# A mixture-of-experts stage on one core: gate and up from split weights to plain fp32, and the context tokens of down on four partition groups

## What is computed

```python
def ec_moe(h, w_router, w_gate, w_up, w_down):
    ...
    cap = EC_CAPACITY_FACTOR * t // N_EXPERTS
    gates, idx = lax.top_k(aff.T, cap)
    xs = ht[idx]
    a = jnp.einsum('ecd,edf->ecf', xs, w_gate)
    u = jnp.einsum('ecd,edf->ecf', xs, w_up)
    y = jnp.einsum('ecf,efd->ecd', jax.nn.silu(a) * u, w_down) * gates[..., None].astype(h.dtype)
    out = jnp.zeros((t, d), h.dtype).at[idx.reshape(-1)].add(y.reshape(-1, d))
```

## Time and profile before

| what | value |
|---|---|
| median of 3 runs | 3486.37 us (3486.07 to 3488.76) |
| profiled execution, span | 3480.6 us |
| PE busy / DVE busy / POOL busy | 3166.9 / 2532.4 / 1483.4 us |
| first transpose of the expert stage | 874.4 us |
| last matmul of the expert stage | 3431.0 us |
| mean granted TensorE clock | 0.949 |

### The profile page before, as it was taken

How to read it: one execution, slowest core, us unless ns; L and a number is a source line. 1 busy time by engine, 2 the same in 40 slices (tenths; PEclk the granted TensorE clock), 3 DMA queues, 4 the chain that set the end, 5 groups by cost and what they waited for, 6 DMA issues and landing times. The chain is left out here.

```text
span 3480.6 us, 50738 instructions
## 1 busy us (share of the span) xinstructions
PE 3166.9 (91%) x19191; PEld 2741.1 (79%) x19191; DVE 2532.4 (73%) x3014; ACT 1278.2 (37%) x2046; POOL 1483.4 (43%) x860
## 2 busy tenths in 40 slices
PE   8999989894899999989898999999898989999994
PEld 2699987683788888878787888888787878888883
DVE  2343331225789898988898898989898989889895
ACT  2222221232334434434343344343434343434432
POOL 2233330123345455453545454544535354535443
PEclk9999999996899999999999999999999999999997
DMA  7311102344667676776767676767667576767673
GB/s 303 114 37 36 38 14 74 117 147 151 205 220 247 210 233 214 223 223 212 238 211 240 221 231 217 236 215 234 220 210 245 195 255 205 245 224 226 218 237 134
DMA packets 483305, 668.23 MB, mean 192 GB/s; under 512 B 14689, under 2 KB 418993, under 8 KB 480050
## 3 DMA queue, kind: packets, MB, share of 16 engines
q1 hardware_dynamic: 476978, 644.45, 55.6%
q0 software_dynamic: 6144, 20.98, 2.5%
HBM read 633.39 MB, written 31.98 MB: 191 GB/s over the span
## 5 line engine op out<-in xcount | busy, mean ns | idle before, releaser
L1202 POOL TENSOR_TENSOR wD_lo<-rawW,wD_hi 128x1024 fp32r<-128x1024 f32 x352 | 960.3, 2759 | 1162.7 <-DVE wD_hi L1541 1162.7
L1401 PE MATMUL psU<-X,wU_hi 128*128 128x320 f32 x2816 | 784.7, 360 | 93.1 <-DVE wU_lo L1202 93.1
L1401 PE MATMUL psG<-X,wG_hi 128*128 128x320 f32 x2816 | 760.9, 352 | 38.2 <-issue 35.1
L1202 DVE TENSOR_TENSOR wU_lo<-rawW,wU_hi 128x1024 fp32r<-128x1024 f32 x350 | 741.2, 2125 | 0.0
L1403 PE MATMUL psU<-X,wU_lo 128*128 128x160 f32 x2816 | 685.0, 243 | 0.0
L1403 PE MATMUL psG<-X,wG_lo 128*128 128x160 f32 x2816 | 677.7, 241 | 0.0
L1401 PEld LDWEIGHTS psU<-X,wU_hi 128*128 128x128 f32 x2816 | 552.7, 196 | 98.6 <-DVE wU_lo L1202 51.0
L1401 PEld LDWEIGHTS psG<-X,wG_hi 128*128 128x128 f32 x2816 | 543.7, 193 | 62.9 <-issue 41.7
L1403 PEld LDWEIGHTS psU<-X,wU_lo 128*128 128x128 f32 x2816 | 562.9, 200 | 0.0
L1403 PEld LDWEIGHTS psG<-X,wG_lo 128*128 128x128 f32 x2816 | 552.5, 196 | 6.4
L1202 DVE TENSOR_TENSOR wG_lo<-rawW,wG_hi 128x1024 fp32r<-128x1024 f32 x350 | 454.6, 1336 | 56.9 <-ACT wG_hi L1208 56.9
(11 more groups left out here) (239 smaller groups left out, 4213.0 us busy)
## 6 DMA issues: line engine op xcount, KB each, us to landing
rawW<-in_w_gate SPq DMA_DIRECT2D x176, 1024.0 KB, 7.4
rawW<-in_w_up SPq DMA_DIRECT2D x176, 1024.0 KB, 8.2
rawW<-in_w_down SPq DMA_DIRECT2D x176, 1024.0 KB, 4.9
wm<-in_w_mod SPq DMA_DIRECT2D x24, 1024.0 KB, 5.0
raw<-in_w_in SPq DMA_DIRECT2D x32, 192.0 KB, 2.4
rawc<-catT SPq DMA_DIRECT2D x10, 512.0 KB, 6.0
acc<-x SPq DMA_DIRECT2D x10, 512.0 KB, 2.7
xn<-xn SPq DMA_DIRECT2D x10, 512.0 KB, 4.1
```

Source lines behind the costliest of these rows:

```text
L1202: eng.tensor_tensor(lo, src, hi.bitcast(F32), ALU.subtract).then_inc(f_lo[kind], 1)
L1401: pe.matmul(out[:, f, 0:2 * C], hi, X[:, k, :], start=(k == 0), stop=False, skip_group_check=True)
```

## The change

Gate and up take the raw fp32 weights and unsplit fp32 tokens in plain fp32 matmuls of 160 columns; their hi and lo parts, `xm`, `gl`, `ga`, `ul`, `ua` and the halves of the split go away. Down keeps split operands for the 128 latent tokens (three products: hi hi, lo hi, hi lo; ACT now makes the hi weights, DVE the lo weights). Its context tokens become plain fp32 matmuls: 32 stationary columns of `hf`, 256 columns of raw down weights each, the four quarters of the output on PSUM partitions 0, 32, 64 and 96. The ring has 4 slots, freed by the matmuls that read them; psG, psU, `sg`, `hf` and `hid` have two buffers; the loop's body holds two experts and returns 6 times, with a hint for the branch; the last down of an expert moves behind the next expert's first gate and up; POOL does no arithmetic.

```diff
-        RING = 3
+        RING = 4
...
-                    def gate_or_up(kind, out, e, i):
-                        s = STEPS * e + i
-                        for k in range(NK):
-                            if k in (0, NK // 2):
-                                pe.wait_ge(f_lo[kind], 2 * s + (1 if k == 0 else 2))
-                            for f in range(2):
-                                hi, lo = (wGU[kind][x][:, k, f * P:(f + 1) * P] for x in range(2))
-                                pe.matmul(out[:, f, 0:2 * C], hi, X[:, k, :], start=(k == 0), stop=False,
-                                          skip_group_check=True)
-                                mm = pe.matmul(out[:, f, 0:C], lo, X[:, k, 0:C], start=False, stop=(k == NK - 1),
+                    def gate_or_up(kind, out, odd, i):
+                        w = raw[:, i % RING, kind, :].rearrange("p (k f) -> p k f", k=NK)
+                        for f in range(2):
+                            for k in range(NK):
+                                mm = pe.matmul(out[:, f, 0:C], w[:, k, f * P:(f + 1) * P], X[:, odd, k, :],
+                                               start=(k == 0), stop=(k == NK - 1), skip_group_check=True)
+                        return mm
+
+                    def down(e, odd, i):
+                        s, q = STEPS * e + i, (odd + i) % 2
+                        if i == 0:
+                            pe.wait_ge(f_y, e)
+                            pe.wait_ge(f_yp, e)
+                        pe.wait_ge(f_hl, s + 1)
+                        for f in range(2):
+                            pe.wait_ge(f_dlo, 2 * s + f + 1)
+                            for h, w in ((0, 0), (1, 0), (0, 1)):
+                                for half in range(2):
+                                    pe.matmul(psS[:, half, :], hid[h][:, q, f, :], wD[w][:, q, f, half * 512:(half + 1) * 512],
...
+                        for f in range(2):
+                            for j in range(4):
+                                mm = pe.matmul(psP[j * CP:(j + 1) * CP, 0:QUAD], hf[:, q, f, CS:C],
+                                               raw[:, i % RING, D_, f * D + j * QUAD:f * D + (j + 1) * QUAD],
...
-                        for i in range(STEPS):
-                            s = STEPS * e + i
-                            if i == 0:
-                                pe.wait_ge(f_x, 2 * e + 2)
-                            pe.wait_ge(f_ga, s + 1)
-                            gate_or_up(G_, psG, e, i).then_inc(f_g, 1)
-                            pe.wait_ge(f_ua, s + 1)
...
+                            raw_ready(pe, G_, e, i)
+                            pe.wait_ge(f_sg, s + 1)
+                            gate_or_up(G_, psG[q], odd, i).then_inc(f_g, 1)
+                            raw_ready(pe, U_, e, i)
+                            pe.wait_ge(f_hf, s + 1)
+                            gate_or_up(U_, psU[q], odd, i).then_inc(f_u, 1)
...
                             if i:
-                                down(e, i - 1)
-                        down(e, STEPS - 1)
+                                down(e, odd, i - 1)
+                            elif not first:
+                                down(e - 1, 1 - odd, STEPS - 1)
...
+                            sp.wait_ge(f_g, s - back + 1)
+                            load(sp, G_, e, i)
+                            sp.wait_ge(f_u, s - back + 1)
+                            load(sp, U_, e, i)
+                            sp.wait_ge(f_d, 2 + s - back + 1)
+                            load(sp, D_, e, i)
...
+                            raw_ready(act, D_, e, i)
+                            act.wait_ge(f_d, s + 1)
+                            for f in range(2):
+                                act.activation(wD[0][:, q, f, :], raw[:, i % RING, D_, f * D:(f + 1) * D],
+                                               ACT.Copy).then_inc(f_dhi, 1)
                             act.wait_ge(f_g, s + 1)
...
+                            dve.tensor_tensor(hf[:, q, :, :], sg[:, q, :, :], psU[q][:, :, 0:C], ALU.mult).then_inc(f_hf, 1)
```

More of the change, by code:

```diff
@@ L1362, in experts @@
             def experts(eng, body):
[L1365 to L1371, removed]
+                body(0, 0, True, False)
+                with nc.Fori(0, E // 2 - 1, engines=(eng.engine,), hint_back_edge=True) as j:
+                    body(2 * j + 1, 1, False, False)
+                    body(2 * j + 2, 0, False, False)
+                body(E - 1, 1, False, True)
             with nc.Block() as block:
@@ L1376, in _, with body @@
                     sp.wait_ge(f_got, 32)
-                    def body(e, first, last):
+                    def body(e, odd, first, last):
                         for i in range(STEPS):
                             s = STEPS * e + i
[L1381 to L1386, removed]
+                            if first and i < RING:
+                                continue
+                            back = RING if i >= RING else STEPS + i - LAST[i]
+                            sp.wait_ge(f_g, s - back + 1)
[4 more added lines that the diff above has]
+                            load(sp, D_, e, i)
                     experts(sp, body)
@@ L1407, in down @@
-                    def down(e, i):
-                        s = STEPS * e + i
-                        pe.wait_ge(f_hl, 1 + s + 1)
-                        if i == 0:
[L1411 to L1422, removed]
@@ L1481, in _ @@
[L1481 to L1496 removed]
+                    act.sem_inc(f_sg, 2)
@@ L1497, in body @@
                             act.wait_ge(f_hf, s + 1)
-                            act.activation(hid[:, i % 2, :, 0:C], hf[:], ACT.Copy).then_inc(f_hh, 1)
-                            if i == STEPS - 1 and not last:
-                                x_hi(e + 1)
-                                hi_halves(act, U_, *n, halves=(1,))
+                            act.activation(sg[:, q, :, :], psG[q][:, :, 0:C], ACT.Silu).then_inc(f_sg, 1)
                             if i == 0 and not first:
-                                take_y(e)
+                                take_context(e)
@@ L1533, in for_scatter @@
                         dve.tensor_copy(gc[:].unsqueeze(2), pair(gT, e - 1)).then_inc(f_si, 1)
-                    def down_hi(e, i, s):
-                        dve.wait_ge(f_d, s + (1 if i else 2))
-                        raw_ready(dve, D_, e, i)
-                        for half in range(2):
-                            dst, src = split_part(D_, i, half, 0)
-                            dve.tensor_copy(dst, src).then_inc(f_hi[D_], 1)
+                        dve.wait_ge(f_si, e)
+                        dve.wait_ge(f_d, 2 + STEPS * e)
@@ new lines, in body @@
+                            dve.tensor_tensor(hid[1][:, q, :, :], hf[:, q, :, 0:CS], hid[0][:, q, :, :].bitcast(F32),
+                                              ALU.subtract).then_inc(f_hl, 1)
+                            if i >= STEPS - NK and not last:
+                                k = i - (STEPS - NK)
+                                dve.wait_ge(f_xt, NK * (e + 1) + k + 1)
+                                x_mod(k, 1 - odd)
+                            if i == 0 and not first:
+                                take_y(e)
```

252 lines of the change are left out of this document (77 added, 175 removed).

## The result

The changed kernel takes 3226.38 us (median of 4 runs, 3223.65 to 3227.82) against 3486.22 us for the kernel before (4 runs, 3485.33 to 3488.76): ratio 0.9257, 95% interval 0.9244 to 0.9271. The profiled execution has a span of 3225.4 us.

A forecast was written before the change was run, and what follows sets the result against it. PE was taken to bound the inside of an expert, something else its ends. 3480.6 + 176 x (P - 1.35) - 193, at P = 2.04, gave 3409, plus 5.8 about 3415 us; range 3355 to 3690.

The forecast's parts named there:

- The failed step: Context part of down: only a quarter's second record and the next quarter's first overlap, nine slots, 1.93 us; chance 0.55.
- P: Time per step of down's context-token matmuls: forecast 2.04 us, break-even 2.45; above 2.45 or under 1.6 means wrong.
- four together: Rival for down's context tokens: records of different partition groups pass a waiting one; P 0.86, about 3207 us, chance 0.13.
- Down, latent 2.84 + P 2.04: Down in each step: twelve unchanged latent matmuls take 2.84 us, the context tokens' plain fp32 matmuls 2.04.
- Gate and up, 64 records: Gate and up in each step: 64 plain fp32 records at 0.137 us take 8.77 us against 8.23, so +0.54.
- Loop returns kept: PE idle where the expert loop returns, 6 times not 13, with its clock cost: bounds 0 and 26 us, 26 kept.
- Transposes a step, with what they add beside them: Two transposes in a step inside an expert: 0.38 us, counted 128 times over the stage.
- Opening of the stage, other small stalls: Loss at the opening of the expert stage: 8 us, expected to stay.
- Profiled execution to median: Distance from the profiled span to the median time: 5.8 us added to the sum.
- I add none: Down: no drain of the engine added for changes of tiling mode, since the timeline showed none between different stationary widths.
- Stalls removed: Expert stage: of 227 us lost, 8 stay at the opening and 26 at loop returns, so 193 go.
- A new wait at the head of an expert: Rival: late down weights stall ACT, `wD_lo`, then down; up to 74 us, 3489 in all; shares the remaining 0.10 chance.

The follow-up runs named there:

- the one with paired blocks: Changed kernel with the context tokens' matmuls of two steps in one block, six blocks an expert instead of eleven: 3200.04 us, ratio 0.9186.

## Why the prediction was wrong

**The failed step: "the second must wait for the first; and in every timeline records start in program order. Then only the second record of a quarter and the first of the next can lie together."** The wait for the own group is real (waves 0.216 us apart, and 3.57 us when all records are on one group). The conclusion from it isn't: a waiting record holds up nobody on another group, as the run with the order of the quarters exchanged shows. So P is not 2.04 but 1.22 (below), under the 1.6 that the prediction named as a sign of being wrong. The rows ahead of the prediction could not have shown otherwise. Their matmuls took the whole array or followed one another in the same group, so "starts in program order" was read from a case where nothing could pass. The rival "four together" is what happened; its P of 0.86 was priced without the ways in and out. The prediction's own sum gives 3050 + 176 x 1.22 + 5.8 = 3270 with the measured P; that is below its range already. The Trainium skill's 2.38 times for three groups (TensorE: Matmul & The Clock Gate, Measured speedup vs the span model) pointed the right way. The trace agrees in kind, with 3.57 / 1.00 us, 3.57 times, for four groups; the estimate of P from that page, 1.44, is above the 1.22 measured.

The other steps, each by its own term (what was forecast, what was measured, and its part of the 189 us between 3415 and 3226):

| Term | Forecast | Measured | us |
|---|---|---|---|
| Down, latent 2.84 + P 2.04 | 4.88 | 3.96 (2184.30 to 2188.26), x 176 | -162 |
| Gate and up, 64 records | 8.77 | 8.69, x 176 | -14 |
| Loop returns kept | 26 | 1.3 waits, no half clock: about 2 | -24 |
| Transposes a step, with what they add beside them | 0.38 | 13.16 - 12.65 = 0.51, x 128 | +16 |
| Opening of the stage, other small stalls | 8 | what remains | +3 |
| Behind the last matmul | 3480.6 - 3431.4 = 49.2 | 3225.4 - 3178.9 = 46.5 | -3 |
| Profiled execution to median | 5.8 | 1.0 | -5 |

- *P* was 1.22 in all, by the kernel without context matmuls: 1.12 of it lies in the 3.96 (2.84 are the latent part), the last 0.10 is the slow first gate record. Four waves at 0.216 are 0.86 of it, the ways in and out the other 0.36. So "I add none" was wrong, too. The Trainium skill's rule that a change of tiling mode drains the engine (TensorEngine Tiling, Key Properties) fits the 0.3 to 0.36 us a block of these runs; that the price is such a drain they don't show. The matmuls of 64 and 32 columns in the earlier trace rows, which showed nothing of the kind, were of split operands. Why those pay nothing and plain fp32 does was not tested.
- *Gate and up* was right: the records lie 0.136 us apart, and 0.137 was forecast from rows of other widths.
- *Stalls removed* was right for DVE's lo halves, `hid` and the ends of experts. The waits are gone from the trace, but no run separates which part of the change removed which: DVE's lighter step, the second buffers, the fourth slot or the down that moved. The gain lies there: the span fell by 255 us, of it 217 by stalls (the 193 of the forecast and 24 at the loop returns) less 3 at the opening, 38 by PE's own steps (176 x 0.31 less 128 x 0.13 beside the transposes: they take 2014.41 to 2014.79, 0.38 as forecast, but gate and up ahead of them take 8.79, not 8.69), and 3 behind the last matmul. The prediction had PE's step growing by 0.69; for this sum the four groups were decisive only by not costing: on one group they cost 446 us and turn the sign.
- *The loop's return*: the bounds 0 and 26 held, the choice of 26 did not. The runs with and without the hint settle it: the hint is worth 51 us in the kernel before and 31 in this one, 5.2 a return where the prediction had 2.47 + 1.8.
- *A new wait at the head of an expert* did not come: no wait of PE for `wD_hi` or `wD_lo` is among its waits, and the transfers are hidden even with 196 us less of matmuls above them.

## What to carry to other kernels

Plain fp32 matmuls with few stationary columns were cheap here when they were spread over four partition groups, in both orders that were tried; on one group they paid the full length of each stream. Gather them into few long blocks, since each block of them among matmuls of the whole array cost 0.3 us or more here. And before a rule on order is taken from a trace, ask whether any row in it had the freedom to break it.

## What the runs showed of the hardware

- Plain fp32 matmuls on four partition groups work at the same time: 16 records of 256 columns in 1.00 us against 3.57 on one group and 1.85 on two; four starts lie 7 ns apart, and 13 ns where each passes three records that wait.
- A block of 32-column plain fp32 matmuls among 128-column ones of split operands costs 0.3 to 0.36 us beside its records; with 128 columns its records and those around it keep their usual distances, to 0.01 us.
- A loop's return without the hint left PE idle for 2.7 us on average in the kernel before (35.1 in 13) and 3.2 in the changed one (19.4 in six), where the granted clock behind the one shown was 0.73; with the hint it was 0.4 us at most in the changed kernel, and 1.5 in the one with paired blocks.
